# A triangular inverse inside a delta-rule kernel: four levels in 32-row blocks on 32x32 TensorE tiles instead of five in 64-row blocks on 64x64 tiles

## The reference, cut to what matters

```python
lmat = jnp.einsum('nbhcd,nbhed->nbhce', kb, k) * decay_strict
eye = jnp.eye(c, dtype=jnp.float32)
tmat = lax.linalg.triangular_solve(lmat + eye, jnp.broadcast_to(eye, lmat.shape),
                                   left_side=True, lower=True, unit_diagonal=True)
u_base = jnp.einsum('nbhce,nbhef->nbhcf', tmat, v * beta[..., None])
w_dec = jnp.einsum('nbhce,nbhed->nbhcd', tmat, kb * jnp.exp(gc)[..., None])
```

## Time and profile before

| | us |
|---|---|
| median of 3 runs | 2191.24 |
| the profiled execution | 2192.85 |
| its span, first to last instruction | 2191.1 |
| TensorE busy | 2144.7 (98%) |
| VectorE, ScalarE, GpSimd busy | 1297.3, 846.1, 219.9 |
| one round of the loop | 66.97 |

### The profile page before, as it was taken

How to read it: one execution, slowest core, us unless ns; L and a number is a source line. 1 busy time by engine, 2 the same in 40 slices (tenths; PEclk the granted TensorE clock), 3 DMA queues, 4 the chain that set the end, 5 groups by cost and what they waited for, 6 DMA issues and landing times.

```text
span 2191.1 us, 49903 instructions
## 1 busy us (share of the span) xinstructions
PE 2144.7 (98%) x18829; PEld 2059.8 (94%) x18829; DVE 1297.3 (59%) x2155; ACT 846.1 (39%) x1674; POOL 219.9 (10%) x313
## 2 busy tenths in 40 slices
PE   6999999999999999999999999999999999999997
PEld 4899999999999999999989999999999999999997
DVE  5556667666776666676675444554565656654443
ACT  3434443344443344433443334433333333343333
POOL 3012111121111121111211001000000000000010
PEclk9999999999999999999999999999999999999999
DMA  5534443444443545434445444444544444454442
GB/s 158 152 108 142 144 138 104 134 144 144 128 137 111 145 142 145 138 104 134 143 147 158 154 154 145 157 151 158 161 149 157 149 157 145 147 169 151 145 142 90
DMA packets 379977, 311.10 MB, mean 142 GB/s; under 512 B 19609, under 2 KB 375866, under 8 KB 379322
## 3 DMA queue, kind: packets, MB, share of 16 engines
q1 hardware_dynamic: 378042, 306.30, 45.8%
q10 hardware_dynamic: 1872, 3.96, 0.5%
HBM read 283.85 MB, written 27.25 MB: 142 GB/s over the span
## 4 chain that ended last, share of the span: by engine, by line
PE 96%; DVE 2%; ACT 1%; issue 1%; DMA 0%; SPq 0%; DVEq 0%; ACTq 0%
PE ps L291 27%; PE ps L293 25%; PE ps L292 25%; PE ps L1131 13%; PE ps L1298 1%; PE ps L1152 1%; ACT zraw L621 0%; DVE wlo L282 0%; DMA xtok<-in_x_sample_dram 0%; DVE sq L826 0%; PE ps L1201 0%; PE ps L1245 0%; PE ps L1194 0%; DVE xlo L820 0%; PE ps L1250 0%
## 5 line engine op out<-in xcount | busy, mean ns | idle before, releaser
L291 PE MATMUL ps<-xhi,whi 128*128 128x320 f32 x3072 | 985.6, 321 | 11.7 <-ACT zraw L621 8.0
L293 PE MATMUL ps<-xhi,wlo 128*128 128x320 f32 x3072 | 951.6, 310 | 0.0
L292 PE MATMUL ps<-xlo,whi 128*128 128x320 f32 x3072 | 951.4, 310 | 0.0
L282 DVE TENSOR_TENSOR wlo<-wraw,whi 128x1024 fp32r<-128x1024 f32 (+1 forms) x484 | 605.8, 1273 | 212.6 <-ACT whi L277 208.9
L291 PEld LDWEIGHTS ps<-xhi,whi 128*128 128x128 f32 x3072 | 579.3, 189 | 35.2 <-issue 27.8
L277 ACT ACTIVATE whi<-wraw 128x1024 fp32r<-128x1024 f32 (+1 forms) x484 | 497.1, 1048 | 263.9 <-PE ps L293 237.1
L292 PEld LDWEIGHTS ps<-xlo,whi 128*128 128x128 f32 x3072 | 579.8, 189 | 0.9
L293 PEld LDWEIGHTS ps<-xhi,wlo 128*128 128x128 f32 x3072 | 578.8, 188 | 0.0
L291 PE MATMUL ps<-bhi,whi 128*128 128x320 f32 x512 | 158.0, 309 | 0.0
L293 PE MATMUL ps<-bhi,wlo 128*128 128x320 f32 x512 | 158.0, 309 | 0.0
L292 PE MATMUL ps<-blo,whi 128*128 128x320 f32 x512 | 158.0, 309 | 0.0
(11 more groups left out here) (333 smaller groups left out, 2310.6 us busy)
## 6 DMA issues: line engine op xcount, KB each, us to landing
wraw<-in_delta_w_in_dram SPq DMA_DIRECT2D x384, 256.0 KB, 3.2
wraw<-in_pool_w_in_dram SPq DMA_DIRECT2D x256, 256.0 KB, 3.0
wraw<-in_delta_w_out_dram SPq DMA_DIRECT2D x128, 256.0 KB, 3.3
wraw<-in_pool_w_out_dram SPq DMA_DIRECT2D x128, 256.0 KB, 3.2
s_s<-in_state_delta_dram SPq DMA_DIRECT2D x32, 512.0 KB, 6.3
out_dram<-s_s SPq DMA_DIRECT2D x32, 512.0 KB, 4.2
wraw<-in_pool_w_group_dram SPq DMA_DIRECT2D x64, 256.0 KB, 3.1
dec<-gc_rows SPq DMA_DIRECT2D x16, 320.0 KB, 4.2
```

The source lines that it names most:

```text
L282: nc.vector.tensor_tensor(wlo[:, slot, 0:width], wraw[:, slot, 0:width], whi[:, slot, 0:width].bitcast(F32), ALU.subtract).then_inc(E("w_l ...
L291: mm(o, whi[:, slot, w], hi[:, k_x, :], start=first, stop=False)
L292: mm(o, whi[:, slot, w], lo[:, k_x, :], start=False, stop=False)
L293: done = mm(o, wlo[:, slot, w], hi[:, k_x, :], start=False, stop=last)
```

## The change: what it does, and the diff

Blocks are 32 rows (`BL = 32`), and `G` has four of them. The tiles `yc`, `xc`, `x0`, `pc`, `level` are 32 wide. Levels 1 to 4 run in the four diagonal 32x32 blocks at once. The level that joins 16-row blocks is the last of them; the next one, k = 5, which joins 32-row blocks to 64-row blocks, is a single off-diagonal 32x32 block for each 64-row half: "lp" for two blocks a unit into partitions 0 and 64, VectorE copies it whole (`p5`), "lxt" for two blocks a unit, and "lx" only for the upper half. X of the upper half is assembled by VectorE in `xm` (64x64), and Y in `ym`: GpSimd multiplies the four blocks of `yc`, repeated along the row, by a block mask (`blocks4`) into the whole 128x128 transposed matrix, and ScalarE then puts the two level-5 blocks into it with two copies. Level 6 reads `ym` and `xm`. VectorE's two copies into `ym` and the semaphore `y_kept` are gone. Setup work on GpSimd for the masks grows (44 selections instead of 26, of smaller pieces).

```diff
-TILE_LEVELS = 6
+TILE_LEVELS = 5
+BL = 32
...
@@ delta_pool, in delta(n, ...), behind the scaling of s_s
+            pool.wait_ge(E("y4"), n)
+            gp.tensor_tensor(ym[:].rearrange("p u (q c) -> p u q c", q=4), yc[:].rearrange("p u (o c) -> p u o c", o=1).to_broadcast(
+                [P, 5, 4, BL]), blocks4[:].rearrange("p (o q) c -> p o q c", o=1).to_broadcast([P, 5, 4, BL]), ALU.mult
+                             ).then_inc(E("ym"), 1)
@@ delta_act
-            for k in range(1, TILE_LEVELS):
+            for k in range(1, TILE_LEVELS + 1):
...
-                    sc.activation(yc[:], blocks(D1[:, 0:320], 5), ACT.Copy).then_inc(E("y1"), 1)
+                    sc.activation(yc[:], blocks(D1[:, 0:160], 5), ACT.Copy).then_inc(E("y1"), 1)
+                elif k < TILE_LEVELS:
+                    sc.activation(half_blocks(yc[:, 0:units, :], k, 1), packed(D1, units, k), ACT.Copy).then_inc(E(f"y{k}"), 1)
                 else:
-                    sc.activation(half_blocks(yc[:, 0:units, :], k, 1), packed(D1, units, k), ACT.Copy).then_inc(E(f"y{k}"), 1)
+                    act.wait_ge(E("ym"), n)
+                    for h in (64, 0):
+                        last = sc.activation(ym[h:h + BL, 0:4, h + BL:h + 64], blocks(D1[h:h + BL, 0:P], 4), ACT.Copy)
+                    last.then_inc(E("y5"), 1)
@@ delta_dve
-            for h in range(2):
-                r = slice(64 * h, 64 * h + 64)
-                last = v.copy_predicated(x0[r, :, :], level[r, 0:1, :].to_broadcast([64, 5, 64]), lmat[r, :, 64 * h:64 * h + 64])
+            for h in range(4):
+                r = slice(BL * h, BL * h + BL)
+                last = v.copy_predicated(x0[r, :, :], level[r, 0:1, :].to_broadcast([BL, 5, BL]), lmat[r, :, BL * h:BL * h + BL])
...
+                else:
+                    v.tensor_copy(p5[:], blocks(D0[:, 0:P], 4)).then_inc(E("p5"), 1)
+                    dve.wait_ge(E("x4"), n)
+                    v.tensor_copy(xm[0:BL, :, 0:BL], xc[0:BL, 0:4, :])
+                    v.tensor_copy(xm[BL:64, :, BL:64], xc[BL:64, 0:4, :])
...
+                    v.tensor_copy(xm[BL:64, :, 0:BL], blocks(D2[BL:64, 0:P], 4)).then_inc(E("x5"), 1)
-            dve.wait_ge(E("y5"), n)
-            for h in range(2):
-                r = slice(64 * h, 64 * h + 64)
-                last = v.tensor_copy(ym[r, :, 64 * h:64 * h + 64], yc[r, :, :])
-            last.then_inc(E("y_kept"), 1)
@@ delta_pe
-            G = (slice(0, 64), slice(64, P))
+            G = [(slice(h, h + BL), h) for h in range(0, P, BL)]
...
-            for k in range(1, TILE_LEVELS):
+            for k in range(1, TILE_LEVELS + 1):
...
-                    for h, r in enumerate(G):
-                        last = one(D0[r, 32 * u:32 * u + 32].rearrange("p (j b) -> p j b", b=1 << k),
-                                   lmat[r, u, 64 * h:64 * h + 64], half_block(yc[r, u, :], k, 1))
+                    for r, h in G:
+                        if k < TILE_LEVELS:
+                            last = one(D0[r, 16 * u:16 * u + 16].rearrange("p (j b) -> p j b", b=1 << k),
+                                       lmat[r, u, h:h + BL], half_block(yc[r, u, :], k, 1))
+                        elif h % 64:
+                            last = one(D0[h - BL:h, BL * u:BL * u + BL], lmat[r, u, h - BL:h], yc[r, u, :])
...
+                        elif k < TILE_LEVELS:
+                            last = one(D1[r, 16 * u:16 * u + 16].rearrange("p (j b) -> p j b", b=1 << k),
+                                       x[r, u, :], half_block(pc[r, k - 1, u, :], k, 1))
+                        elif h % 64 == 0:
+                            last = one(D1[r, BL * u:BL * u + BL], x[r, u, :], p5[r, u, :])
...
+                        elif h == 0:
+                            last = one(D2[BL:64, BL * u:BL * u + BL], p5[r, u, :], x[r, u, :])
...
-                last = one(D0[0:64, 64 * u:64 * u + 64], lmat[64:P, u, 0:64], yc[64:P, u, :])
+                last = one(D0[0:64, 64 * u:64 * u + 64], lmat[64:P, u, 0:64], ym[64:P, u, 64:P])
...
-                last = one(D1[0:64, 64 * u:64 * u + 64], xc[0:64, u, :], p6[0:64, u, :])
+                last = one(D1[0:64, 64 * u:64 * u + 64], xm[0:64, u, :], p6[0:64, u, :])
...
-            pe.wait_ge(E("y_kept"), n)
```

More of the change, by code:

```diff
@@ L90, in build @@
     mask_s = place(m, "mask_s", [P])
-    level = place(m, "level", [TILE_LEVELS, 64], U8)
+    level = place(m, "level", [TILE_LEVELS, BL], U8)
     seqmask = place(m, "seqmask", [NSEQ])
@@ L117, in build @@
     uc = list(a)
-    yc = place(a, "yc", [5, 64])
-    xc = place(a, "xc", [5, 64])
+    yc = place(a, "yc", [5, BL])
+    xc = place(a, "xc", [5, BL])
+    p5 = place(a, "p5", [4, BL])
     udm = place(uc, "udm", [4, P])
+    a[0] = max(a[0], uc[0])
     amat = place(a, "amat", [5, P])
@@ L139, in build @@
     kq_m = place(a, "kq_m", [4 * P + 32])
-    x0 = place(a, "x0", [5, 64])
-    pc = place(a, "pc", [TILE_LEVELS - 1, 5, 64])
+    x0 = place(a, "x0", [5, BL])
+    pc = place(a, "pc", [TILE_LEVELS - 1, 5, BL])
     ym = place(a, "ym", [5, P])
+    xm = place(a, "xm", [4, 64])
+    blocks4 = place(a, "blocks4", [4, BL])
     g = [shared]
@@ L150, in build @@
     crow = place(g, "crow", [2, P])
-    lv = place(g, "lv", [TILE_LEVELS, 64])
+    lv = place(g, "lv", [TILE_LEVELS, BL])
     tri_p = place(g, "tri_p", [P])
@@ L253, in packed @@
     def packed(v, n, k):
-        return v[:, 0:32 * n].rearrange("p (u j b) -> p u j b", u=n, b=1 << k)
+        return v[:, 0:16 * n].rearrange("p (u j b) -> p u j b", u=n, b=1 << k)
     def pool_strips(t, skip, take):
@@ L476, in delta_pool @@
                     else:
-                        v = lv[r, k, 0:32].rearrange("p (j r) -> p j r", r=b)
+                        v = lv[r, k, 0:16].rearrange("p (j r) -> p j r", r=b)
                         base, pattern, cm = ((0, [[-2 * b, n], [0, b]], 1), (b - 1, [[2 * b, n], [0, b]], -1))[step]
                     keep_where(v, v, base, pattern, cm, 0.0).then_inc(E("consts"), 1)
-            pool.wait_ge(E("consts"), 20 + (12, 24, 26)[step])
+            pool.wait_ge(E("consts"), 20 + (20, 40, 44)[step])
         gp.tensor_copy(level[:], lv[:]).then_inc(E("c_all"), 1)
         gp.memset(kq_m[:], 0.0)
-        gp.memset(ym[:], 0.0).then_inc(E("consts"), 1)
+        gp.memset(blocks4[:], 1.0)
+        gp.memset(xm[:], 0.0).then_inc(E("consts"), 1)
         pool.wait_ge(E("c_all"), 1)
-        pool.wait_ge(E("consts"), 47)
-        for h in range(2):
-            r = slice(64 * h, 64 * h + 64)
[L488 to L492, removed]
+        pool.wait_ge(E("consts"), 65)
+        keep_where(blocks4[:], blocks4[:], 0, [[-BL, 4], [0, BL]], 1, 0.0).then_inc(E("consts"), 1)
+        pool.wait_ge(E("consts"), 66)
+        keep_where(blocks4[:], blocks4[:], BL - 1, [[BL, 4], [0, BL]], -1, 0.0).then_inc(E("consts"), 1)
+        pool.wait_ge(E("consts"), 67)
+        for h in range(4):
+            r = slice(BL * h, BL * h + BL)
+            unit = ident[r, BL * h:BL * h + BL].rearrange("p (o c) -> p o c", o=1)
+            gp.tensor_copy(x0[r, :, :], unit.to_broadcast([BL, 5, BL])).then_inc(E("consts"), 1)
+            pool.wait_ge(E("consts"), 68 + 2 * h)
+            gp.tensor_copy(pc[r, :, :, :].rearrange("p k u c -> p (k u) c"), unit.to_broadcast([BL, 20, BL])).then_inc(E("consts"), 1)
+            pool.wait_ge(E("consts"), 69 + 2 * h)
         pool.wait_ge(E("x_lo"), KT)
@@ L707, in delta @@
             act.wait_ge(E("xt"), n)
-            sc.activation(yc[:], blocks(D1[:, 0:320], 5), ACT.Copy).then_inc(E("y0"), 1)
+            sc.activation(yc[:], blocks(D1[:, 0:160], 5), ACT.Copy).then_inc(E("y0"), 1)
             split(4)
-            for k in range(1, TILE_LEVELS):
+            for k in range(1, TILE_LEVELS + 1):
                 units = 5 if k < S_LEVELS else 4
@@ L1010, in delta @@
                 if k == 1:
-                    v.tensor_copy(xc[:], blocks(D2[:, 0:320], 5))
-                elif k < 5:
+                    v.tensor_copy(xc[:], blocks(D2[:, 0:160], 5))
+                elif k < 4:
                     v.tensor_copy(half_blocks(xc[:, 0:units, :], k, 0), packed(D2, units, k))
-                else:
-                    v.tensor_copy(half_blocks(xc[:, 0:units, :], k, 0), packed(D2, units, k)).then_inc(E("x5"), 1)
-            dve.wait_ge(E("y5"), n)
-            for h in range(2):
-                r = slice(64 * h, 64 * h + 64)
-                last = v.tensor_copy(ym[r, :, 64 * h:64 * h + 64], yc[r, :, :])
-            last.then_inc(E("y_kept"), 1)
+                elif k == 4:
+                    v.tensor_copy(half_blocks(xc[:, 0:units, :], k, 0), packed(D2, units, k)).then_inc(E("x4"), 1)
+                else:
+                    v.tensor_copy(xm[BL:64, :, 0:BL], blocks(D2[BL:64, 0:P], 4)).then_inc(E("x5"), 1)
             conv_next(1, 0)
@@ L1274, in delta @@
             for u in range(5):
-                for h, r in enumerate(G):
```

(17 more changed lines are left out.)

15 lines of the change are left out of this document (8 added, 7 removed).

## The result

The changed kernel takes 2259.69 us (median of 4 runs, 2252.77 to 2266.5) against 2191.29: ratio 1.031, 95% interval 1.0293 to 1.0325. It is slower by 3.1%, where 2148 was forecast. Its profiled execution took 2252.77 us, the fastest of the four.

A forecast was written before the change was run, and what follows sets the result against it. TensorE's queue was taken to bound the kernel (PE busy 98%). Savings of (2.55 + 0.13) x 16 rounds = 42.9 us took the profiled 2192.85 to 2149.9, less 1.6 for the median: 2148 us, range 2136 to 2184.

The forecast's parts named there:

- Step 1: Inverse's runs behind a fill: 98 slots a round fall from 0.059 to 0.033 us on narrower tiles, saving 2.55 us.
- Rival A: Inverse's small matmuls: a slot has a floor, 0.052 to 0.059 us, giving 2178 to 2189 us; chance 0.11.
- rival C: Inverse's small matmuls: instruction issue bounds the run, 15 ns each, 5 us a round more, about 2270 us; chance 0.03.
- Step 2: lx runs: shorter slots gain nothing, ACT's copies decide; net 0.13 us less a round, with 0.19 more at level 5.
- Step 3: GpSimd's assembly of `ym` before level 6: 1.57 us, bounds 1.1 and 3.2, within 2.85 us of room, costing nothing.
- The sum of steps 1 and 2: Inverse in each round: 2.55 + 0.13 us saved, 42.9 us over 16 rounds.
- What may be given back: instructions: Section on TensorE's loop body growing by 456 instructions, seven blocks to 8 or 9; how many fit was not shown.
- rival B: Jump back at round's end: body leaves the buffer, 3.7 + 2.8 us a round, 2239 us, chance 0.11; short stops 0.09.
- the hidden case: TensorE's loop: instruction loads cost PE nothing; the forecast of 2138 to 2164 us had 0.62.

The follow-up runs named there:

- the earlier signal: Written-out changed kernel with one projection piece moved, ScalarE signalling level 5 after the first of its two copies: 2160.33 us; without the moved piece 2165.77 us.
- the second shifted kernel: Changed kernel with 42 one-column matmuls (168 instructions) more ahead of TensorE's loop, so the loop starts 119 instructions into a block: 2189.25 us.

## Why the prediction was wrong

- **What bounds the kernel**: right. TensorE's queue decides, and a gap on it is paid in full.
- **Step 1, the slot**: right. 0.033 us was taken, 0.034 measured: 8 instructions in 34 ns. Rival A (a floor at 0.052 to 0.059) and rival C (15 ns an instruction) fall, and so does what was put beside A, that narrow tiles would gain little.
- **Step 2, the lx runs hidden behind ACT**: right for levels 1 to 4, 0.44 us at level 3 against 0.41 worked out. At level 5 the two copies take 0.55 us, 0.08 more than taken; PE stands 0.58 us there each round, of which the earlier signal gave back 0.27 (4.4 / 16).
- **Step 3, GpSimd's assembly**: right, 1.57 us in the trace as taken and not waited for:

```profile
152.70 1.57 POOL L551 TENSOR_TENSOR ym<-yc,blocks 128x640 f32<-128x640 f32 x1 [7.71 <-ACT yc L730]
```

- **The sum of steps 1 and 2**, 2.68 us a round: 2.54 measured in a round without a stop; of the 0.14 missing, 0.08 is level 5's copies. Over 16 rounds that would be 40.6 us in place of 43. No kernel shows it whole: the best one is 31 us below the kernel before.
- **What failed** is "What may be given back: instructions". It entered the sum with nothing, and its long form, rival B, had a chance of 0.11. What the runs showed in its place is 7.3 us for each repeated round: 71.69 us in the changed kernel against 64.43 in a round without a stop. Writing the loop out gave back 91 us, 6.5 us a jump. The section had the growth of the body (456 instructions more; the program has 1497 and 1953), the seven blocks, and the absence of loads before; it left the room in the buffer open and then took the hidden case as the likeliest. The reason given, "a load takes 1.1 us, and the round ends in projection matmuls already queued", covers one load. In the trace PE stood 1.1 us after that queue ran out, and again for the next block, 49 instructions on.
- **Rival B** named place and mechanism. Its price, 3.7 us of stops and 2.8 of clock, 6.5 us a round, was near the 7.3 measured, but that is luck in part: both terms were taken from a single wait of another kind, for VectorE, and the rows before could not show the price of a reload. Measured are 1.27 + 2.44 us of stops at the start of the round and 1.4 + 0.3 in the level-2 stretch, 5.4 together, which leaves 1.9 for the half clock. Rival B's time was 2239; 2260 was measured.

The rule of the Trainium skill that was quoted ("Runtime: NRT & Kernel Launch", Instruction fetch mechanics) gives 2048 instructions, eight blocks, as TensorE's buffer, and a wait at a jump out of the window. It spoke for rival B, and the wait at the jump is there. The measurements differ from it in two points, and they decide. The Trainium skill gives the window there as two pages; by that the jump back would have to wait in a body of seven blocks too, and it does not. And by a buffer of eight blocks the two bodies that touch eight (1953 and 1601 instructions) would fit, but they are loaded anew.

For a reader the mistake is one of weighing: an unknown with a sharp edge (fits or does not) was given the chance of a mild disturbance, though the body would pass from seven blocks to nine, and the only thing in favour of its staying was that nothing in the trace denied it.

## What to carry to other kernels

Count instructions in a hardware loop's body as a resource. Where the trace shows no instruction loads in a loop, find out how many blocks the body touches before adding to it. Past seven blocks of 256 on TensorE, write the loop out (91 us here), or place its start early in a block: 23 or 119 instructions into one in place of 207 gave 62 and 70 us here. Smaller tiles cut the time of a slot nearly in proportion to their width (0.111, 0.060 and 0.034 us for 128, 64 and 32), but here twice as many instructions stood in each slot of the smaller tiles. And a run that is waited out behind another engine's copy gives nothing.

## What the runs showed of the hardware

- An fp32 matmul of the code is four instructions of TensorE's program (two weight loads and two matmuls in the trace). A block is 16 KB (2.16 MB in 132), and with the loops written out 14 rounds of 1953 and 1497 instructions load 107 and 81 of them: 256 and 259 instructions each.
- Residence is sharp: 1577 instructions in seven blocks, 2199.84 us and no load in the loop; 1601 in eight, 2265.59 us and all blocks loaded in each round.
- Behind a jump to a block that is gone TensorE stood 1.1 to 1.3 us on average. Where 49 instructions lay between the target and the next block it stood another 2.4 us there, and where 137 or 233 did it did not stand.
- Straight code is not free either. With 32-column tiles, where a few hundred instructions run within 2 to 3 us, TensorE stood for up to 1.7 us in some rounds of the written-out kernels, 7 to 12 us in all, with no releaser in the profile; with 64-column tiles, written out, it never did. That it stood for its program is argued from where these stops lie, not shown by a record of its own.
- The changed kernel, with stops of 1.3, 2.4 and 1.4 us in a repeated round, had a granted clock of 0.97 over these rounds; the second shifted kernel, with stops of 1.1 and 0.5 us kept 1.00, the level of 2.4 GHz.
